# Experts' down projection from rounded high and low parts: high parts by ScalarE, low parts in place by GpSimd and VectorE in halves

## What is computed

```python
act = jax.nn.silu(jnp.einsum("nd,edf->nef", xt, w1)) * jnp.einsum("nd,edf->nef", xt, w3)
```

## Time and profile before

| | us |
|---|---|
| median of 3 runs (2360.01 to 2363.82) | 2363.68 |
| the profiled execution | 2361.83 |
| its span in the profile | 2360.1 |
| PE busy in the span | 2223.3 (94%) |
| VectorE busy | 1404.1 (59%) |
| ScalarE busy | 1082.0 (46%) |
| GpSimd busy | 346.5 (15%) |

### The profile page before, as it was taken

How to read it: one execution, slowest core, us unless ns; L and a number is a source line. 1 busy time by engine, 2 the same in 40 slices (tenths; PEclk the granted TensorE clock), 3 DMA queues, 4 the chain that set the end, 5 groups by cost and what they waited for, 6 DMA issues and landing times.

```text
span 2360.1 us, 32542 instructions
## 1 busy us (share of the span) xinstructions
PE 2223.3 (94%) x12005; PEld 1863.0 (79%) x12005; DVE 1404.1 (59%) x2174; ACT 1082.0 (46%) x1863; POOL 346.5 (15%) x431
## 2 busy tenths in 40 slices
PE   7899999999999999899999999999989997989997
PEld 6788878888887888688888889977778886857774
DVE  5657446777777655653343445758646757366665
ACT  4455445766666434532233314644333353345552
POOL 1000001121111000000000002942334430011011
PEclk9999999999999999999999999999989999899999
DMA  5221522232223523223232313131010033359995
GB/s 199 79 88 24 107 92 70 62 92 67 70 62 129 178 68 111 90 92 105 90 107 89 107 55 126 59 103 45 19 45 1 1 108 107 145 216 406 418 404 194
DMA packets 169179, 273.23 MB, mean 116 GB/s; under 512 B 9865, under 2 KB 142297, under 8 KB 159193
## 3 DMA queue, kind: packets, MB, share of 16 engines
q1 hardware_dynamic: 164585, 255.22, 32.1%
q0 software_dynamic: 4464, 16.25, 1.8%
HBM read 240.00 MB, written 31.46 MB: 115 GB/s over the span
## 4 chain that ended last, share of the span: by engine, by line
PE 78%; DVE 8%; ACT 6%; DVEq 3%; issue 2%; POOL 1%; DMA 1%; POOLq 1%; ACTq 0%; SPq 0%
PE ps L184 19%; PE ps L186 18%; PE ps L185 18%; PE ps L3775 3%; ACT pair L371 1%; PE ps L3194 1%; PE ps L3177 1%; PE ps L1141 1%; DVE pair L377 1%; PE ps L1678 1%; PE ps L1700 1%; PE ps L3739 1%; PE ps L3145 1%; PE ps L2775 1%; PE ps L1119 1%
## 5 line engine op out<-in xcount | busy, mean ns | idle before, releaser
L186 PE MATMUL ps<-pair,pair 128*128 128x512 f32 (+1 forms) x2216 | 798.5, 360 | 0.0
L184 PE MATMUL ps<-pair,pair 128*128 128x512 f32 (+1 forms) x1960 | 725.7, 370 | 35.7 <-DVE pair L430 8.7
L185 PE MATMUL ps<-pair,pair 128*128 128x512 f32 (+1 forms) x1960 | 725.6, 370 | 0.0
L186 PEld LDWEIGHTS ps<-pair,pair 128*128 128x128 f32 x2216 | 422.6, 191 | 63.5
L184 PEld LDWEIGHTS ps<-pair,pair 128*128 128x128 f32 x1960 | 374.8, 191 | 95.9 <-issue 29.9
L185 PEld LDWEIGHTS ps<-pair,pair 128*128 128x128 f32 x1960 | 374.1, 191 | 63.5 <-issue 7.2
L377 DVE TENSOR_TENSOR pair<-ring,pair 128x2048 fp32r<-128x2048 f32 x95 | 219.1, 2306 | 163.9 <-ACT pair L371 163.7
L371 ACT ACTIVATE pair<-ring 128x2048 fp32r<-128x2048 f32 x102 | 194.7, 1909 | 199.3 <-PE ps L186 188.1
L1912 DVE SCALAR_TENSOR_TENSOR arena<-arena 128x512 f32<-128x512 f32 x128 | 98.0, 766 | 21.5 <-issue 12.1
L184 PE MATMUL ps<-part,pair 128*128 128x512 f32 x256 | 102.6, 401 | 6.3 <-DVE part L3549 4.9
L184 PE MATMUL ps<-pair,ring_rounded 128*128 128x512 f32 x256 | 102.0, 398 | 3.3 <-DVE ring_rounded L1900 2.3
(11 more groups left out here) (556 smaller groups left out, 3812.3 us busy)
## 6 DMA issues: line engine op xcount, KB each, us to landing
ring<-in_w_in SPq DMA_DIRECT2D x54, 1024.0 KB, 6.6
arena<-in_w_exp_down SPq DMA_DIRECT2D x23, 1024.0 KB, 10.6
ring<-in_w_up SPq DMA_DIRECT2D x16, 1024.0 KB, 5.5
ring<-in_w_down SPq DMA_DIRECT2D x16, 1024.0 KB, 5.1
ring<-in_w_exp_gate SPq DMA_DIRECT2D x16, 1024.0 KB, 8.4
ring<-in_w_exp_up SPq DMA_DIRECT2D x16, 1024.0 KB, 10.7
expert_results<-arena SPq DMA_DIRECT2D x22, 512.0 KB, 11.0
ring<-in_w_in SPq DMA_DIRECT2D x16, 512.0 KB, 6.1
```

The source lines that it names most:

```text
L184: nc.tensor.matmul(out, lhs[1], rhs[0], start=start, stop=False)
L185: nc.tensor.matmul(out, lhs[0], rhs[1], start=False, stop=False)
L186: return nc.tensor.matmul(out, lhs[0], rhs[0], start=False, stop=stop)
```

## The change

The down product now is made from rounded parts as well. `down` calls `product`, so it issues twelve fp32r matmuls in place of the four float32 calls. Its parts are made like this, a tile t at a time:

- `down_hi(t)` (new, L3874 in the changed file): ScalarE copies the landed down matrix (128x2048) into its high part. There is one buffer of high parts for all tiles, so this waits until the down product of tile t - 1 is done, and until the matrix has landed.
- `down_rest`: the low part is the difference of raw matrix and high part, written over the raw matrix. The first half (128x1024) is made by GpSimd (`down_lo`, behind the gather of tile t + 3 in its queue), the second half by VectorE (L3913 in the changed file). Both wait for `down_hi(t)`.
- The hidden rows get a high part by ScalarE, in the instruction that copied them before, and a low part by VectorE (`act_lo`, L4108), which is a new instruction.
- `down(t)` waits for both halves of the low weights and for the low part of the hidden rows.
- `last_tile` is no longer spread over gathers 4, 6 and 8, but runs as one piece behind gather 1, and the first `down_hi` waits for it since the buffer of high parts lies on its data.

The diff, cut to what the stage does (the rest moves buffers in SBUF):

```diff
@@ -3606,8 +3610,9 @@
             small = xT.rearrange("p c t -> p (c t)")
             silu = [small[:, i * DE:(i + 1) * DE] for i in range(2)]
             act = [small[:, (2 + i) * DE:(3 + i) * DE] for i in range(2)]
-            actT = [small[:, (4 + i) * DE:(5 + i) * DE].rearrange("p (k n) -> p k n", k=2) for i in range(2)]
-            y = [small[:, (6 + 4 * i) * DE:(10 + 4 * i) * DE] for i in range(2)]
+            actP = [core.pair_of(x_at + (4 + 2 * i) * DE, x_at + (5 + 2 * i) * DE, 2, P) for i in range(2)]
+            y = [small[:, (8 + 4 * i) * DE:(12 + 4 * i) * DE] for i in range(2)]
+            downP = [core.pair_of(core.lists_at - 2048, down_at + 2048 * i, 2, D) for i in range(2)]
             last_parts, last_turned, second_diag = (h_tok[:, 2 + i // 2, i % 2 * 512:(i % 2 + 1) * 512]
                                                     .rearrange("p (t n) -> p t n", t=NT) for i in range(3))
             last_share = h_tok[:, 3, 512:512 + 2 * NT]
@@ -3632,6 +3637,7 @@
             w2v = IN["w_exp_down_2"][0].rearrange("e (p k) n -> e p k n", p=P)
             wg = IN["w_router_group_2"][0].rearrange("(k p) n -> p k n", p=P)
             we = IN["w_router_expert_2"][0].rearrange("(k p) n -> p k n", p=P)
+            down_high, low_halves, down_low = (Signal(s.sem, s.base + n) for s, n in ((gained, DC), (in_var, 1), (consts, 2)))
             before = len(stages)
             split_before = core.slots
 
@@ -3757,23 +3763,24 @@
                 def turn_act(i):
                     pe.wait_ge(*act_made.at(i + 1))
                     if i:
-                        pe.wait_ge(*act_copied.at(i))
+                        pe.wait_ge(*low_halves.at(2 * i))
                     for k in range(2):
                         mm = nc.tensor.transpose(ps[:, 4, k * P:(k + 1) * P],
                                                  act[i % 2].rearrange("p (m k) -> p k m", k=2)[:, k, :], core.ident)
                     mm.then_inc(act_turned.sem, 1)
 
                 def down(i):
-                    pe.wait_ge(*act_copied.at(i + 1))
-                    pe.wait_ge(s_down[i % 2], 16 * (i // 2 + 1))
+                    pe.wait_ge(*down_low.at(i + 1))
+                    pe.wait_ge(*low_halves.at(2 * i + 2))
                     if i:
                         pe.wait_ge(*y_act.at(i))
                         pe.wait_ge(*y_dve.at(i))
-                    w = down_raw[i % 2].rearrange("p (k n) -> p k n", k=2)
+                    a, w = actP[i % 2], downP[i % 2]
                     for half in range(2):
                         for k in range(2):
-                            mm = nc.tensor.matmul(ps[:, 5 + half, :], actT[i % 2][:, k, :],
-                                                  w[:, k, half * 512:(half + 1) * 512], start=k == 0, stop=k == 1)
+                            at = slice(half * 512, (half + 1) * 512)
+                            mm = product(nc, ps[:, 5 + half, :], (a.hi[:, k, :], a.lo[:, k, :]),
+                                         (w.hi[:, k, at], w.lo[:, k, at]), start=k == 0, stop=k == 1)
                     mm.then_inc(down_made.sem, 1)
 
                 def turn_last_parts():
@@ -3860,24 +3867,34 @@
                     a.wait_ge(*up_made.at(t + 1))
                     a.activation(silu[t % 2], ps[:, 2 + t % 2, 0:DE], ACT.Silu).then_inc(silu_made.sem, 1)
 
+                def down_hi(i):
+                    if not i:
+                        a.wait_ge(*consts.at(2))
+                    a.wait_ge(s_down[i % 2], 16 * (i // 2 + 1))
+                    a.activation(downP[i % 2].hi, down_raw[i % 2].rearrange("p (k n) -> p k n", k=2), ACT.Copy)\
+                        .then_inc(down_high.sem, 1)
+
                 weights_hi(0)
                 rows_hi_(0)
                 weights_hi(1)
                 for t in range(TILES + 1):
                     if t:
                         a.wait_ge(*act_turned.at(t))
-                        a.activation(actT[(t - 1) % 2], ps[:, 4, 0:DE].rearrange("p (k n) -> p k n", k=2), ACT.Copy)\
+                        a.activation(actP[(t - 1) % 2].hi, ps[:, 4, 0:DE].rearrange("p (k n) -> p k n", k=2), ACT.Copy)\
                             .then_inc(act_copied.sem, 1)
                     if t < LAST:
                         gate_hidden(t)
                         rows_hi_(t + 1)
                     if t:
                         a.wait_ge(*down_made.at(t))
+                    if t < TILES:
+                        down_hi(t)
+                    if t == LAST:
+                        gate_hidden(t)
+                    if t:
                         if t >= 3:
                             a.wait_ge(s_y[(t - 1) % 2], 16 * ((t - 1) // 2))
                         a.activation(y[(t - 1) % 2][:, 0:512], ps[:, 5, :], ACT.Copy).then_inc(y_act.sem, 1)
-                    if t == LAST:
-                        gate_hidden(t)
                     if t == LAST - 7:
                         a.wait_ge(*sums_made.at(2))
                         a.activation(last_turned.rearrange("p t n -> p (t n)"), ps[:, 7, :], ACT.Copy).then_inc(exps.sem, 1)
@@ -3890,6 +3907,11 @@
                     if t % 2:
                         a.wait_ge(*var_made.at(t // 2 + 1))
                         a.activation(root[:, t - 1:t + 1], var[:, t - 1:t + 1], ACT.Sqrt).then_inc(root_made.sem, 1)
+
+            def down_rest(eng, i, k):
+
+                return eng.tensor_tensor(downP[i % 2].lo[:, k, :], down_raw[i % 2][:, k * D:(k + 1) * D],
+                                         downP[i % 2].hi[:, k, :].bitcast(F32), ALU.subtract)
 
             def row_max(dve, dst, src):
                 dve.tensor_reduce(dst, src, AX.X, ALU.max)
@@ -4081,7 +4103,14 @@
                     dve.tensor_tensor(act[t % 2], silu[t % 2], ps[:, 2 + t % 2, DE:2 * DE], ALU.mult)\
                         .then_inc(act_made.sem, 1)
 
+                def act_lo(i):
+                    dve.wait_ge(*act_copied.at(i + 1))
+                    dve.tensor_tensor(actP[i % 2].lo, ps[:, 4, 0:DE].rearrange("p (k n) -> p k n", k=2),
+                                      actP[i % 2].hi.bitcast(F32), ALU.subtract).then_inc(low_halves.sem, 1)
+
                 for t in range(TILES + 1):
+                    if t:
+                        act_lo(t - 1)
                     if t < LAST:
                         gated(t)
                         rows_lo(t + 1)
@@ -4090,6 +4119,9 @@
                         if t >= 3:
                             dve.wait_ge(s_y[(t - 1) % 2], 16 * ((t - 1) // 2))
                         dve.tensor_copy(y[(t - 1) % 2][:, 512:1024], ps[:, 6, :]).then_inc(y_dve.sem, 1)
+                    if t < TILES:
+                        dve.wait_ge(*down_high.at(t + 1))
+                        down_rest(dve, t, 1).then_inc(low_halves.sem, 1)
                     if t == LAST:
                         gated(t)
                     if t + 2 < TILES:
@@ -4145,21 +4177,22 @@
                 gp.drain().then_inc(consts.sem, 1)
                 flat_share = share.rearrange("p n t -> p (n t)")
 
-                def last_tile(i):
-
-                    if i == 4:
-                        gp.tensor_tensor(last_share, in_tile[:, :, LAST], flat_share, ALU.mult)
-                        gp.drain()
-                        gp.tensor_tensor(of_slot, of_slot, last_share.unsqueeze(2).to_broadcast([P, 2 * NT, P]), ALU.mult)
-                    if i == 6:
-                        gp.drain()
-                        gp.tensor_tensor(flat_share, flat_share, last_share, ALU.subtract)
-                        gp.tensor_tensor(last_parts, of_slot[:, 0:NT, :], of_slot[:, NT:2 * NT, :], ALU.add)
-                    if i == 8:
-                        gp.drain()
-                        gp.tensor_tensor(second_diag, core.ident.unsqueeze(1).to_broadcast([P, NT, P]),
-                                         share[:, 1, :].unsqueeze(2).to_broadcast([P, NT, P]), ALU.mult)
-                        gp.drain().then_inc(consts.sem, 1)
+                def last_tile():
+
+                    gp.tensor_tensor(last_share, in_tile[:, :, LAST], flat_share, ALU.mult)
+                    gp.drain()
+                    gp.tensor_tensor(of_slot, of_slot, last_share.unsqueeze(2).to_broadcast([P, 2 * NT, P]), ALU.mult)
+                    gp.drain()
+                    gp.tensor_tensor(flat_share, flat_share, last_share, ALU.subtract)
+                    gp.tensor_tensor(last_parts, of_slot[:, 0:NT, :], of_slot[:, NT:2 * NT, :], ALU.add)
+                    gp.drain()
+                    gp.tensor_tensor(second_diag, core.ident.unsqueeze(1).to_broadcast([P, NT, P]),
+                                     share[:, 1, :].unsqueeze(2).to_broadcast([P, NT, P]), ALU.mult)
+                    gp.drain().then_inc(consts.sem, 1)
+
+                def down_lo(i):
+                    gp.wait_ge(*down_high.at(i + 1))
+                    down_rest(gp, i, 0).then_inc(down_low.sem, 1)
 
                 gp.wait_ge(rows_stored, 16 * NT)
```

(17 more changed lines are left out.)

## The result

The change costs 4.8%: the median of 4 runs is 2475.77 us (2474.55 to 2477.97), against 2362.16 of 4 runs of the kernel before beside them, a ratio of 1.0481 with a 95% interval of 1.0465 to 1.0498. The profiled execution took 2474.55 us with a span of 2472.8, so 112.7 us of span to account for. The prediction said slower and named the ring that is lengthened, but put the time at 2447 and at 2466 at most, 10 us under what was measured.

The account below looks back on a forecast made before the run. PE was taken to bound the kernel, a down product every 10.08 us. Twenty tiles at 14.05 add 79.4, with 3 and 2.8 at the ends 85, giving 2447 us; range 2408 to 2466.

Parts of the forecast that it names:

- the ring: Closed loop from down(t-1) through down_hi, weights_hi, weights_lo and act_lo to down(t); forecast 14.05 us a tile, before 10.08.
- What would show it: Signs for right, among them down products every 13 to 15 us and a loop clock under 1.00; signs for wrong.
- PE's clock: Down product behind PE's new idle stretch partly runs at half clock: 0.8 us a tile, between 0 and 2.4.
- the sum: Twenty tiles at 14.05 instead of 10.08 us, 79.4, with 3 and 2.8 at the ends: 85 us more, 2447.
- Ends of the loop: Before the loop, the first down_hi waits for last_tile, 3 us (0 to 6); behind the loop 2.8 us.
- worse: Rival: the clock falls for longer than the product, the up product runs out of cover; 15.5 a tile, 2476; chance 0.10.
- What the new queue costs: ScalarE's and VectorE's queues delay act_lo, so down(t) starts 9.15 us after down(t-1) ends and ends at 12.05.
- GpSimd's half: down_lo on GpSimd and VectorE's low parts exclude each other, moving act_lo by 1.2 us a tile, between 0 and 2.4.
- Edits that cost nothing: Transfers, down load and the GpSimd and SyncE queues add nothing; the down load lands after 10.6 us, inside 14.05.
- A clock that stays at 1.00: Rival: exclusion of GpSimd and VectorE holds but PE's clock does not fall; 13.25 us a tile, 2431; chance 0.20.
- Little exclusion: Rival: GpSimd and VectorE hardly disturb each other; 12.05 to 12.9 us a tile, 2407 to 2424; chance 0.17.
- PE stays the bound: Faster rival: everything else fits under PE's 9.4 us a tile, so the saving shows; 2355 us; chance 0.05.

Follow-up runs that it names:

- clock_kept: The changed kernel with three float32 matmuls a tile, their result unread, added in PE's idle stretch between transposes and down product; 2437.52 us.
- act_low_between: The changed kernel with VectorE making the low part of the hidden rows between its two weights_lo instructions instead of behind both; 2399.11 us.
- low_all_vector: The changed kernel with VectorE making both halves of the low down weights and GpSimd none; 2441.84 us.
- down_load_first: act_low_between with SyncE issuing the down load of tile t+1 ahead of the gate and up loads it was queued behind; 2389.04 us.

## Why the prediction was wrong

Direction, ring and links were right, and of the signs that "What would show it" lists for right only the pace failed (15.21 us for 13 to 15). **The step that failed is "PE's clock"**, as a size. It took 0.8 us between bounds of 0 and 2.4, "as the fall need not meet the product in full". It meets it in full in about every second tile (5.46) and for about two thirds of it in the others (4.6). The product takes 4.94 instead of the 3.7 of the sum, 1.2 more, and clock_kept, where it takes 2.97 behind an unchanged wait, shows that all of it is the clock: 20 x 1.16 = 23 of the 28 us that were missing. "Ends of the loop" is most of the rest. The sum rested on one stretch of 2.8 us at half clock behind one idle stretch. In the loop the idle stretch comes back in every tile, and products of 5.46 and some 4.6 us take turns. The row of a single event gave the level and not the duration. The prediction's own working from it gave 1.3, and the 0.8 went under that by no row; with 1.3 the sum would have been 2457. The measured cost is 1.97 (4.94 for 2.97), nearer to the upper bound, which was worked out from the pace of the earlier trace rows. With that bound the ring is 15.65 and the time 2479, so the range ended inside the bounds of its own step.

The rival "worse" (ring 15.5, 2476) has the right time by luck: its ring is 0.3 too long, its ends are 4 us too short, and its reason is not there. The up product had cover enough: the transposes behind it end 6.6 to 7.0 us after the down product, 6.62 before the change (7.3 and 7.1 in the tile that also transposes the last tile's parts), so the half clock reached it by 0.4 us at most, and PE then stood idle for 3.0 us or more in every tile.

- **"What the new queue costs"**: right. 10.27 from product to product against 10.35, each link within 0.1 us of the forecast but for GpSimd's part.
- **"GpSimd's half"**: right. Forecast 1.2, measured 1.08 (5.57 instead of 4.49) and 1.07 by taking it away. The rule of the Trainium skill that was weighed there (SBUF — State Buffer, Who interferes with whom) decided for the right value: GpSimd's half takes 3.45 behind VectorE's and 2.37 in the first tile, where it did not have to wait, and VectorE's next one, 1.22 us short of GpSimd's end when it begins (2233.38 and 2231.15 + 3.45), is 1.08 longer. Which of the two goes first did not follow that rule in the first tile (last section).
- **"Edits that cost nothing"**: right at this ring. The down load lands after 7.6 us, ahead of need. That it "would be the next wait" with a ring near 10.6 came true at 11, in act_low_between.
- **"Ends of the loop"**: the wait of ScalarE was sized well (2.73 for 3), but I counted it alone. The twenty rings are counted from the end of the first down product, and the first tile has its own `down_hi`, its own exclusion and its own half clock ahead of that end: 7.4 instead of 3. Behind the loop 2.5 for 2.8.
- **Rivals.** A clock that stays at 1.00 gives 13.25 by the prediction and 13.23 in clock_kept. Little exclusion is refuted by the 1.07 of low_all_vector. "PE stays the bound" asked for what act_low_between and down_load_first did, and even with GpSimd's half gone as well the second ring held 10.63. Behind it stood the transfers, which allow no less than 9.93 in the long run.

No version here beats the kernel before. The best one is 0.7% slower.

## What to carry to other kernels

Where a change puts an idle stretch like those here (2.6 and 3.65 us) ahead of a product in every pass, price that product with half of it to all of it at half clock, as it came out here in all but one of the tiles (4.3 to 5.46 for 2.97), and let the range reach the whole. Follow the queue of the engine that feeds the new wait to its end before moving one instruction: here the new order exposed the late down load, and all three repairs together (order, load, engine) exposed a second ring. And a kernel whose transfers already fill the loop can be paid for saved PE time only until their lead is used up, so look at that first.

## What the runs showed of the hardware that I had not expected

- One idle stretch of 2.48 us ahead of a product left the clock up; one of 2.6 on average in each tile did not (low_all_vector, 0.88 over the loop), and one of about 1.1 did (act_low_between, 0.99). The length alone does not tell: in act_low_between the product behind 2.06 us (2173.17) took 3.00 and the one behind 1.99 us (2267.28) took 4.58, and in the change two products behind 3.69 us (2209.05 and 2223.66) took 4.34 and 5.45.
- In the first tile VectorE's `weights_lo` began at 2109.88, GpSimd's half 0.26 later and right behind the issue of a gather on GpSimd. GpSimd's took 2.37 as if alone, and VectorE's pair lasted 2.5 longer. Here the one that began first was the one that waited, against the order that the rule of the Trainium skill under "GpSimd's half" gives, and it was so in clock_kept and act_low_between too (VectorE 0.24 and 0.25 ahead). Why was not tried.
- GpSimd's first large instruction behind two gathers began 7.64 us after the small one ahead of it. Between them stands a drain, and it ended 0.13 us after the gather issued ahead of it had landed (2099.36 and 2099.23), by the same 0.13 in the six kernels built on the change, and by 0.26 in the kernel before (2120.07 and 2119.81), where the earlier trace rows has 6.76. So the drain lasted until the gather had landed; that it waits for the transfer was not tested by an edit.
